# Layer norm statistics of a tile's first half made behind that half's sum in the two output projections, kept in a row of slots

## The reference

```python
def layer_norm(x, g, b):
    xf = x.astype(F32)
    mu = jnp.mean(xf, axis=-1, keepdims=True)
    var = jnp.mean(jnp.square(xf - mu), axis=-1, keepdims=True)
    y = (xf - mu) * lax.rsqrt(var + LN_EPS)
    return (y * g.astype(F32) + b.astype(F32)).astype(x.dtype)
...
    if layer < N_A_LAYERS:
        y = mlstm_mixer(u, a_w_in[layer], a_b_gates[layer], a_norm_w[layer], a_w_out[layer])
    else:
        q = rope_partial((u @ b_w_q[j]).reshape(B, S, A_HEADS, A_HEAD_DIM), positions)
        y = swa_sink_attention(q, k_sh, v_sh, b_sinks[j]) @ b_w_o[j]
    h = layer_norm(DEEPNORM_ALPHA * h + (1 + g_m) * y, ln_g[2 * layer], ln_b[2 * layer])
    u = modulate(h, sh_f, sc_f)
    y = jnp.square(jax.nn.relu(u @ mlp_w_up[layer])) @ mlp_w_down[layer]
    h = layer_norm(DEEPNORM_ALPHA * h + (1 + g_f) * y, ln_g[2 * layer + 1], ln_b[2 * layer + 1])
```

## Time and profile before

| | |
|---|---|
| median of 3 runs | 2303.83 us (2303.28 to 2304.91) |
| the profiled execution's own time | 2304.14 us |
| its span, first to last instruction | 2302.4 us |
| PE busy | 2225.0 us (97%) |
| DVE busy | 1249.9 us (54%) |
| ACT busy | 684.9 us (30%) |
| POOL busy | 179.8 us (8%) |
| mean granted PE clock | 0.992 |

### The profile page before, as it was taken

How to read it: one execution, slowest core, us unless ns; L and a number is a source line. 1 busy time by engine, 2 the same in 40 slices (tenths; PEclk the granted TensorE clock), 3 DMA queues, 4 the chain that set the end, 5 groups by cost and what they waited for, 6 DMA issues and landing times. The chain is left out here.

```text
span 2302.4 us, 28097 instructions
## 1 busy us (share of the span) xinstructions
PE 2225.0 (97%) x10398; PEld 1817.8 (79%) x10398; DVE 1249.9 (54%) x2121; ACT 684.9 (30%) x1312; POOL 179.8 (8%) x207
## 2 busy tenths in 40 slices
PE   4999999999999999999999999999999999999997
PEld 3788888777888888888887866677788888888886
DVE  7324556578546445455567565757743443443447
ACT  2311444162202213113145455636130221221221
POOL 0000221010000000000012023322000000000003
PEclk9999999999999999999999999999999999999999
DMA  6444553304133233232222100211120210210211
GB/s 250 121 125 119 117 125 109 100 28 127 57 99 118 66 108 100 81 110 83 90 83 94 37 29 21 81 56 37 55 83 19 64 60 22 64 55 27 64 37 74
DMA packets 49696, 183.96 MB, mean 80 GB/s; under 512 B 6400, under 2 KB 6576, under 8 KB 49104
## 3 DMA queue, kind: packets, MB, share of 16 engines
q1 hardware_dynamic: 42768, 161.50, 22.2%
q0 software_dynamic: 6096, 21.16, 3.9%
q10 hardware_dynamic: 752, 0.22, 0.0%
HBM read 174.43 MB, written 8.42 MB: 79 GB/s over the span
## 5 line engine op out<-in xcount | busy, mean ns | idle before, releaser
L1597 PE MATMUL ps<-uhi,whi 128*128 128x512 f32 x1152 | 453.2, 393 | 14.0 <-DVE ulo L1251 6.3
L1599 PE MATMUL ps<-uhi,wlo 128*128 128x512 f32 x1152 | 450.9, 391 | 0.0
L1598 PE MATMUL ps<-ulo,whi 128*128 128x512 f32 x1152 | 450.8, 391 | 0.0
L1597 PE MATMUL ps<-whi,hhi 128*128 128x512 f32 x1024 | 401.1, 392 | 5.3 <-DVE resid L1374 5.3
L1599 PE MATMUL ps<-whi,hlo 128*128 128x512 f32 x1024 | 399.5, 390 | 0.0
L1598 PE MATMUL ps<-wlo,hhi 128*128 128x512 f32 x1024 | 399.3, 390 | 0.0
L1374 DVE TENSOR_TENSOR resid<-ps,resid 128x512 f32<-128x512 f32 x256 | 176.6, 691 | 359.9 <-PE ps L1599 343.4
L832 ACT ACTIVATE h_whole<-ps 128x512 f32<-128x512 f32 x128 | 76.4, 597 | 833.0 <-PE ps L1599 833.0
L1597 PE MATMUL ps<-whi,uhi 128*128 128x512 f32 x704 | 289.3, 411 | 6.6 <-DVE resid L1287 4.7
L1006 DVE TENSOR_TENSOR wlo<-stage,whi 128x1024 fp32r<-128x1024 f32 x180 | 219.6, 1224 | 112.7 <-ACT whi L654 112.7
L1599 PE MATMUL ps<-whi,ulo 128*128 128x512 f32 x704 | 276.2, 392 | 0.0
(11 more groups left out here) (227 smaller groups left out, 2086.6 us busy)
## 6 DMA issues: line engine op xcount, KB each, us to landing
stage<-in_stream SPq DMA_DIRECT2D x276, 512.0 KB, 3.6
aux<-in_early SPq DMA_DIRECT2D x2, 2048.0 KB, 10.8
early_place<-in_early SPq DMA_DIRECT2D x2, 2048.0 KB, 20.3
resid<-in_xt SPq DMA_DIRECT2D x8, 512.0 KB, 24.9
resid<-in_x POOLq DMA_DIRECT2D x8, 512.0 KB, 9.4
resid_dram<-resid POOLq DMA_DIRECT2D x8, 512.0 KB, 3.0
resid<-resid_dram POOLq DMA_DIRECT2D x8, 512.0 KB, 3.6
out<-resid SPq DMA_DIRECT2D x8, 512.0 KB, 2.6
```

Source lines behind the costliest of these rows:

```text
L1597: pe.matmul(dst, left_hi, right_hi, start=start, stop=False)
L1598: pe.matmul(dst, left_hi, right_lo, start=False, stop=False)
L1599: return pe.matmul(dst, left_lo, right_hi, start=False, stop=stop)
```

## The change

The statistics of the first half of each tile are made in the first pass, right behind that half's sum, with a wait for the sum. The second pass makes only those of the second half. `stats` becomes a row of 12 slots of 6 numbers: tile t's first half writes slot t + 1, its second half slot t, and `bn_aggr` reads both. For the norms behind the MLPs both halves are still made together; the wait for `xhat_ready` now stands between their `bn_stats` and `bn_aggr`. The numbers of `bn_stats` (64) and `bn_aggr` (32) stay the same. The names `sumsq`, `factor`, `mean` and `r`, which the mLSTM keeps in `stats`, stay at the same offsets; what lies behind `stats` in memory moves by 192 bytes per partition.

```diff
-        stats = sb("stats", [P, 2, 12])
+        stats = sb("stats", [P, 72])
...
-            def norm(ln, t):
-
-                j = t % 2
+            def half_stats(t, half):
+
+                at = 6 * (t + 1 - half)
+                return v.bn_stats(stats[:, at:at + 6], resid[:, t, half * HALF:(half + 1) * HALF])
+
+            def norm(ln, t, halves=(0, 1)):
+
+                for half in halves:
+                    step.mark(half_stats(t, half))
                 if t >= LAG:
 
                     v.wait_ge(xhat_ready, T * ln + t - 1)
-                for half in range(2):
-                    step.mark(v.bn_stats(stats[:, j, 6 * half:6 * half + 6],
-                                         resid[:, t, half * HALF:(half + 1) * HALF]))
-                v.bn_aggr(moments[:, j, :], stats[:, j, :]).then_inc(moments_ready, 1)
+                v.bn_aggr(moments[:, t % 2, :], stats[:, 6 * t:6 * t + 12]).then_inc(moments_ready, 1)
...
                 add_out(FIRST["out0"] + t, t, 0, ALPHA)
+                v.wait_ge(dve_evac, DVE_BEFORE[FIRST["out0"] + t] + 1)
+                step.mark(half_stats(t, 0))
...
-                norm(0, t)
+                norm(0, t, (1,))
...
                 add_out(FIRST["op0"] + t, t, 0, 1.0)
+                v.wait_ge(dve_evac, DVE_BEFORE[FIRST["op0"] + t] + 1)
+                step.mark(half_stats(t, 0))
...
-                norm(2, t)
+                norm(2, t, (1,))
```

More of the change, by code:

```diff
@@ L288, in build @@
         nmr = sb("nmr", [P, 2, 1])
-        sumsq, factor, mean = stats[:, 1, 4:4 + H], stats[:, 1, 0:H], stats[:, 0, H:2 * H]
+        sumsq, factor, mean = (stats[:, n:n + H] for n in (4 * H, 3 * H, H))
         with ExitStack() as a:
@@ L1173, in _ @@
             preps(18, 19)
-            r = stats[:, 0, 0:H]
+            r = stats[:, 0:H]
             def take_raw(c, pair):
```

## The result

The kernel after takes 2310.71 us at the median (2309.48 to 2314.08, 8 runs), the kernel before 2303.93 us in the same job (2302.32 to 2304.91, 8 runs): ratio 1.0028, 95% interval 1.0019 to 1.0037. The change is slower by 6.8 us, where 2304.1 was forecast with 2307.0 as the upper end. The profiled execution has a span of 2307.7 us against 2302.4; mean granted clock 0.993 against 0.992.

What follows compares the result with a forecast made beforehand. PE, busy in 97% of the span, was taken as the bound. Terms -0.57 + 0 + 1.39 - 0.57 = +0.25 us gave 2304.4 on the profiled execution, 2304.1 against the median; range 2301.8 to 2307.0.

Steps and rivals of the forecast that it cites:

- The first MLP's start: PE's 0.57 us wait at the first MLP product vanishes as DVE drops statistics; the same at the second MLP.
- Pair 10: Attention's last pairs, in op0: an inserted statistic delays `totals` and so POOL; PE waits about 0.75 us.
- pair 11: Next attention pair in op0: the inserted statistic is hidden, and PE's 0.20 us wait before its scores is won.
- tile 6 of `op0`: Its insertion stands before `preps(114, 115)`, and the whole 0.84 us goes onto a PE wait of 0.51 us.
- out0: Stage with 8 inserted statistics, hidden behind loads and DVE's waits for PE: cost 0, at worst up to 0.84 us once.
- The price of an insertion: A wait and a `bn_stats` put behind an add cost DVE 0.71 + 0.73 - 0.60 = 0.84 us.
- The lock between DVE and POOL: Two-input DVE instructions and POOL's SBUF reads exclude each other; in pair 11 DVE's operation slips ahead, winning 0.20 us.
- Rival 1: POOL starts first in pair 11 and PE's scores wait 0.84 us: +1.04 us, 2305.1 us; chance 0.22.
- Rival 3: The attention loop is a closed ring without DVE room; each insertion from pair 10 lengthens its pair: +4.8, 2308.6; chance 0.08.
- pairs 12 to 14: Attention pairs in op0 where DVE's 1.90 us wait for ACT hides insertions: 0, at most 0.1 us each for two pairs.
- Nothing beyond: Behind each MLP's first product no further gain: the 3.15 us wait stays and moves with PE.
- norms 1 and 3: Norms with the same instructions and only a moved wait; DVE idled 2.2 us before all 64 `bn_stats`: 0.

Runs made afterwards that it cites:

- e1: The whole change, with smaller and merged buffers keeping every operand at its address in the kernel before: 2304.54 us, ratio 0.9999 to the kernel before.
- e2: The kernel before with only the unused buffer `pad`, ahead of `qk`, `hhi` and `hlo`, made 192 bytes larger: 2310.82 us, ratio 1.0026.
- e4: The kernel before with an unused 192-byte buffer ahead of `uhi`, so all six operands move together: 2303.92 us, ratio 0.9999.
- e9: The kernel before with 256 bytes of small buffers allocated ahead of `whi`, so `whi` and `wlo` move by 256: 2307.22 us, ratio 1.0005.
- e5: The kernel before with `pad`, ahead of `hhi` and `hlo`, made 64 bytes larger: 2324.17 us, ratio 1.0088.
- e3: The kernel before with `pad`, ahead of `hhi` and `hlo`, made 128 bytes larger: 2321.28 us, ratio 1.0067.
- e6: The kernel before with 128 bytes ahead of `whi`, moving `whi`, `wlo`, `hhi`, `hlo` but not `uhi`, `ulo`: 2331.98 us, ratio 1.0114.

## Why the prediction was wrong

**What held.** The local terms held in their places, sign and mechanism. The first MLP's start won 0.80 and the second's 0.81, where 0.57 each was forecast. The 0.57 is what stands in brackets in the row, counted from the modelled end of the transposes at 1583.08; start to start the second MLP's product followed them after 1.60 us before and 0.79 after, and that is the size to use. Pair 10 cost 0.72 (forecast 0.75), pair 11 gave back 0.20, tile 6 of `op0` cost 0.76 (forecast 0.84), out0 nothing. They add up to -0.80 + 0.72 - 0.20 + 0.76 - 0.81 = -0.33 us against the forecast +0.25. The price of an insertion of 0.84 us, which came from the row spacing of 0.71 behind a waited add and not from the 0.60 that follows from the Trainium skill's page "VectorE: DVE Perf Modes", section "The DRAIN you can't avoid", shows once more in pair 10: `totals` releases POOL at 1471.99, 2.39 later than in the earlier trace rows, of which 1.52 is PE's shift by then, so 0.87.

The lock between DVE and POOL went as worked out: short in pair 11 (0.15), and in pair 12 a row of 0.96, which ends at 1496.38 with POOL's, 1494.47 + 1.88 = 1496.35. PE never waited for that one. Rival 1, with the lock in pair 11, did not occur. Rival 3, the closed ring, named the right side and nearly the right time (2308.6) by a mechanism that is not there: no wait of 0.8 in pairs 12 to 14, and e1 has all its insertions and is not slower.

**What failed.** The step is the term for the inside of the MLPs, which the sum puts at nothing: "Nothing beyond" and "It moves with PE" for what lies behind the first product of each MLP, and 0 for norms 1 and 3. The MLPs were taken as work that the change does not touch, since it adds no instruction and no wait there. But the change makes `stats` 192 bytes longer. The section on the change says that what lies behind it moves by 192 bytes, and the prediction gives that no cost and no reason for none. It puts `hhi` and `hlo` 192 bytes (modulo 256) from `whi` and `wlo`, and the steps of 3072 matmuls of a kernel that PE bounds become 2.1 ns longer in the mean, 6.4 us. The measured 6.8 is 6.4 with the local -0.3 and some scatter (the medians' runs spread over 2.6 and 4.6 us). No rival had it, and the large products of before could not have given its size, because all their operands stand at distance 0 there; e2, a single number changed, would have measured it.

e1 takes the placement away and leaves the change, e2 does the placement alone, and the two results (0.9999 and 1.0026 against 1.0028 of the change) are what makes this shown and not argued. What the hardware does inside with two addresses that differ modulo 256 stays open, as do why 64 costs more than 192 and why at 192 the three steps are unequal (231.7, 229.2, 225.8 ns); and distances that are not a multiple of 64 were not tried.

## What to carry to other kernels

A change of a buffer's size is a change of the addresses of all that is allocated behind it. In a kernel bound by PE, work out where the streamed operands and the weights of the large products come to lie before and after, and keep them a multiple of 256 bytes apart; or look first at the spacing of matmuls in a stretch that the change does not touch, since 1% there appears in no list of waits, and in the groups only as 3 to 5 ns of a mean of 390. And before an effect is looked for in the order of the work, run the old kernel with only the placement changed.

## What the runs showed of the hardware

The spacing of 128x512 matmuls at full clock (2.4 GHz), by the distance between the streamed operand and the weights in SBUF modulo 256 bytes, worked out as above:

| distance | second halves, ns | from | kernel's excess |
|---|---|---|---|
| 0 | 226.7 to 226.9 | before, e1, e4, e9 | |
| 64 | 233.3 | e5 | 19 us |
| 128 | 232.4 | e3 (e6 in the first halves 233.2) | 16 us |
| 192 | 228.9, a mean of unequal steps | after, e2 | 6 to 7 us |

The second and fourth columns agree with 3072 matmuls: 3072 x 6.5 ns = 20, x 5.6 = 17, x 2.1 = 6.4 us.

The Trainium skill's page "SBUF — State Buffer", section "Who interferes with whom", gives TensorE two independent read ports, one for the moving operand and one for the weights, and says that only the port pair shared by DVE and GpSimd causes contention. For the pair the trace agrees (the 0.96 us row above). For TensorE these runs differ: with the same instructions the spacing goes from 226.7 to 233.3 ns with nothing but the buffers' places changed (e2, e3, e5). The measurement decides: where the two operands lie matters to TensorE's pace. Which of its reads hold each other up is not shown.
